# Sixteen more tokens leave the dense expert path of a mixed layer kernel: 352 columns, 160 dots, a new order of gathers

## What is computed

```python
s = jnp.einsum('thpd,hpkd->thpk', q, sub_keys)            # scores against 2 x 128 keys per head
s_top, i_top = lax.top_k(s, PEER_TOPK)                     # 16 of each half
best_s, best_pos = lax.top_k(cand_s, PEER_TOPK)            # 16 of the 256 pairs
experts = jnp.take_along_axis(cand_i, best_pos, axis=-1)
g = jax.nn.softmax(best_s, axis=-1)
act = jax.nn.gelu(jnp.einsum('thkd,td->thk', expert_u[experts], xb))
wgt = (g * act)
y = jnp.einsum('thk,thkd->td', wgt, expert_v[experts])
```

## Time and profile before

| | |
|---|---|
| median of 3 runs | 2411.23 us (2410.53 to 2413.74) |
| profiled execution, first to last instruction (the span) | 2411.4 us |
| TensorE busy | 2367.4 us (98%) |
| VectorE busy | 1567.8 us (65%) |
| GpSimd busy | 1244.2 us (52%) |
| bytes moved by DMA | 526.14 MB, mean 218 GB/s |

### The profile page before, as it was taken

The page is one execution under the profiler, slowest core; times in us unless marked ns, Lnnn a source line. Parts: engine busy times, 40 slices in busy tenths (PEclk is TensorE's granted clock), DMA queues, the critical chain, the costliest instruction groups (busy, mean ns, idle before and its releaser), DMA issues.

```text
span 2411.4 us, 35928 instructions
## 1 busy us (share of the span) xinstructions
PE 2367.4 (98%) x12892; PEld 2127.2 (88%) x12892; DVE 1567.8 (65%) x2831; ACT 945.5 (39%) x1488; POOL 1244.2 (52%) x704
## 2 busy tenths in 40 slices
PE   7999999999999999999999999999999999999998
PEld 4878887899999999999999999997777888888886
DVE  5258535689899999779999999892266225422201
ACT  4374333344455555333333333342353223332312
POOL 2305443337899999555555555444304444444443
PEclk9999999999999999999999999999999999999999
DMA  7227522327978898999999999943202222222231
GB/s 283 80 115 258 182 91 84 133 94 255 324 252 301 299 328 309 396 379 414 416 415 409 417 408 414 370 166 106 82 14 96 97 96 96 96 93 99 90 102 70
DMA packets 179613, 526.14 MB, mean 218 GB/s; under 512 B 18240, under 2 KB 70896, under 8 KB 178224
## 3 DMA queue, kind: packets, MB, share of 16 engines
q1 hardware_dynamic: 120928, 345.24, 39.7%
q0 software_dynamic: 43024, 159.14, 17.0%
q10 hardware_dynamic: 15552, 20.36, 2.4%
HBM read 474.93 MB, written 49.73 MB: 218 GB/s over the span
## 4 chain that ended last, share of the span: by engine, by line
PE 91%; DVE 3%; DMA 2%; issue 2%; POOL 1%; ACT 1%; SPq 0%; ACTq 0%; DVEq 0%; POOLq 0%
PE bank L1372 21%; PE bank L1374 21%; PE bank L1373 21%; PE pair L1373 6%; PE pair L1372 6%; PE pair L1374 6%; PE pair L1726 1%; POOL wlo L714 1%; DMA wraw<-in_w 1%; PE bank L1889 1%; PE pair L1513 1%; PE bank L1552 1%; PE bank L1539 1%; DMA act_dram<-actb 1%; PE pair L1664 1%
## 5 line engine op out<-in xcount | busy, mean ns | idle before, releaser
L714 POOL TENSOR_TENSOR wlo<-wraw,whi 128x1024 fp32r<-128x1024 f32 x303 | 740.4, 2446 | 761.1 <-ACT whi L856 760.2
L1372 PE MATMUL bank<-HH,whi 128*128 128x512 f32 (+1 forms) x2048 | 740.2, 361 | 9.5 <-DMA T<-in_keys 3.0
L1373 PE MATMUL bank<-HL,whi 128*128 128x512 f32 (+1 forms) x2048 | 735.8, 359 | 0.0
L1374 PE MATMUL bank<-HH,wlo 128*128 128x512 f32 (+1 forms) x2048 | 735.7, 359 | 0.0
L856 ACT ACTIVATE whi<-wraw 128x1024 fp32r<-128x1024 f32 x456 | 481.8, 1058 | 632.2 <-PE pair L1374 337.4
L1372 PEld LDWEIGHTS bank<-HH,whi 128*128 128x128 f32 x2048 | 385.0, 188 | 54.8 <-issue 5.7
L1374 PEld LDWEIGHTS bank<-HH,wlo 128*128 128x128 f32 x2048 | 384.5, 188 | 40.3
L1373 PEld LDWEIGHTS bank<-HL,whi 128*128 128x128 f32 x2048 | 385.0, 188 | 39.6 <-issue 0.5
L780 POOL DMA_INDIRECT VROW<-in_w,which x128 | 206.0, 1609 | 190.5 <-DVE YROW L2522 178.0
L2454 DVE TENSOR_TENSOR wlo<-wraw,whi 128x1024 fp32r<-128x1024 f32 x153 | 186.4, 1219 | 20.9 <-ACT whi L856 20.0
L773 POOL DMA_INDIRECT X<-in_u_rows,which x128 | 149.0, 1164 | 57.3 <-DVE dots L2296 32.6
(11 more groups left out here) (447 smaller groups left out, 3815.1 us busy)
## 6 DMA issues: line engine op xcount, KB each, us to landing
wraw<-in_w SPq DMA_DIRECT2D x456, 512.0 KB
gate_dram<-GS SPq DMA_DIRECT2D x24, 1024.0 KB
GJ<-gate_dram SPq DMA_DIRECT2D x32, 768.0 KB
act_dram<-actb ACTq DMA_DIRECT2D x108, 184.0 KB
AJ<-act_dram SPq DMA_DIRECT2D x108, 184.0 KB
adaw<-in_ada SPq DMA_DIRECT2D x32, 512.0 KB
ada<-in_ada SPq DMA_DIRECT2D x16, 512.0 KB, 14.2
NB<-in_nab POOLq DMA_DIRECT2D x4, 1024.0 KB
```

What stands on the lines that cost most here:

```text
L714: nc.gpsimd.tensor_tensor(wlo[:, slot, :, :].rearrange("p k c -> p (k c)"), wraw[:, slot, :, :].rearrange("p k c -> p (k c)"), whi[:, slot ...
L1372: pe.matmul(out_, ah, bh, start=first, stop=False, **kw)
L1373: pe.matmul(out_, ah, bl, start=False, stop=False, **kw)
L1374: return pe.matmul(out_, al, bh, start=False, stop=last, **kw)
```

## The change

Sixteen more tokens of the block before the last go by rows. `FT` is 32, so `SD` = 352, `STEPS` = 88, `FS` = 4 and `DOTS` = 160: a row of V for the few tokens after each third tile instead of each seventh. Of the 160 dots, 28 stay in the lead, 44 are in the gate stage (46 before), `TAIL_DOTS` = 66 in the tail (38 before) and 22 in the second stage (32 before), one in five tiles. The tail's dots are spread over the 25 tiles 103 to 127. In its first 12 tiles (103 to 114) the low halves are made by GpSimd, which puts the gathers of each tile behind them; from tile 115 on (`U_POOL`) VectorE makes them. The number of slots stays four.

```diff
-FT = 16
+FT = 32
...
-U_POOL = 4 * GATE_IT + GATE_TILES + 3
+U_TAIL = 4 * GATE_IT + GATE_TILES + 3
+U_POOL = 115
...
-GATE_DOT = 2
-PSUM_DOTS = TOP_DOTS + STEPS // GATE_DOT
-U_DOTS = 112
+GATE_DOTS = 44
+PSUM_DOTS = TOP_DOTS + GATE_DOTS
+TAIL_DOTS = 66
+U_DOTS = PSUM_DOTS + TAIL_DOTS
 DOTS = P + FT
-V_DOT_TILES = [10 * m // 3 + 1 for m in range(32)][:DOTS - U_DOTS]
+V_DOT_TILES = [5 * m + 1 for m in range(DOTS - U_DOTS)]
...
+        def gate_dots(q):
+
+            return GATE_DOTS * q // STEPS
+
...
@@ GpSimd, gate stage and tail
-                if q >= 2 * GATE_DOT and q % GATE_DOT == 0:
+                while fetched < R + TOP_DOTS + gate_dots(max(q - 2, 0)):
                     fetch_u(fetched)
                     fetched += 1
             for t in range(lows, U_POOL):
                 lo(G0["U"] + t, t % R)
-            for k in range(fetched, U_DOTS + R):
+                while fetched < R + PSUM_DOTS + (t - U_TAIL + 1) * TAIL_DOTS // (P - U_TAIL):
+                    fetch_u(fetched)
+                    fetched += 1
+            u_fetches = min(U_DOTS + R, DOTS)
+            for k in range(fetched, u_fetches):
                 fetch_u(k)
@@ VectorE, gate stage
-                if q % GATE_DOT == GATE_DOT - 1:
+                while dotted[0] < TOP_DOTS + gate_dots(q + 1):
                     dot()
@@ VectorE, tail
-            v.wait_ge(w_lo, G0["U"] + U_POOL)
-            tail_dots = U_DOTS - PSUM_DOTS
-            for t in range(U_POOL, P):
-                lo(G0["U"] + t, t % R)
-                while dotted[0] < PSUM_DOTS + (t - U_POOL + 1) * tail_dots // (P - U_POOL):
+            for t in range(U_TAIL, P):
+                if t == U_POOL:
+                    v.wait_ge(w_lo, G0["U"] + U_POOL)
+                if t >= U_POOL:
+                    lo(G0["U"] + t, t % R)
+                while dotted[0] < PSUM_DOTS + (t - U_TAIL + 1) * TAIL_DOTS // (P - U_TAIL):
                     dot()
```

More of the change, by code:

```diff
@@ L820, in _ @@
                 pool.wait_ge(g_out[b], 64 * TD)
-            fetched = U_DOTS + R
+            fetched = u_fetches
             for n, k in enumerate(V_ROWS):
```

## The result

The changed kernel takes 2462.86 us (median of 4 runs, 2460.47 to 2466.33), the kernel before 2411.28 us beside it (2410.53 to 2413.74). The ratio is 1.0212 with a 95% interval of 1.0197 to 1.0226: slower by 51.6 us, where +33.5 was forecast. Direction and range held; the likeliest value was 18 us too low.

A forecast was written before the change was run, and what follows sets the result against it. TensorE looked like the bound (98% busy), but DMA was taken to give at most 410 to 416 GB/s. From 2411.4 us, -3.5 - 8 + 41 + 4 = +33.5 gives 2445 us; range 2418 to 2480.

The forecast's parts named there:

- The lead and the gate stage: Before the tail: lead -3.5 us (bounds 0 and -6.2), gate stage -8 us (bounds -4 and -12).
- The second stage: Second expert stage: DMA at its limit, 4.09 us a tile for tiles 0 to 95, in sum +4 us.
- TensorE's pace: Rival, second stage: it keeps 3.84 us a tile, -20.5 us in place of +4, whole 2421 us; chance 0.15.
- a slot bound of 4.3 us a tile: Rival, second stage: slots of V rows bind it, +24 us, whole 2465 us; chance 0.16.
- The tail: Last VectorE gate sum to second stage: gathers wait for slots, 2.3 us a dot, 153 us, +41 us.
- the low bound: Tail: round of a less loaded DMA, 8.0 us, 2.0 a dot, 134 us, under the limit of bytes.
- the high bound: Tail: GpSimd's 12 low halves (29 us) stand between its gathers with nothing hiding them, 182 us.
- The signs: Expected: tail some 150 us, TensorE idle a third, dots 2.2 to 2.4 us apart, DMA near 400 GB/s.
- the third: Sign of being wrong: TensorE's waits in the tail bring its clock to 1.2 GHz, 7.7 us a tile, tail over 190.

The follow-up runs named there:

- ScalarE's order: Changed kernel, but ScalarE evacuates TensorE's first-stage tiles 125 to 127 before it splits the second stage's first three products: 2459.60 us.
- The square of four runs: Changed kernel 2462.86 us; with the tail's low halves all on VectorE 2446.68; with `few_x` in PSUM for dots 72 to 103 2449.43; with both 2444.22.
- the split of 38/50: Changed kernel with 38 dots in the tail, 50 in the second stage and all the tail's low halves on VectorE: 2431.16 us, ratio 1.0074.

## Why the prediction was right, and where it was too low

The direction and the path to it were right: the tail decides, by gathers that wait for slots. The size of that one term was too small.

**The lead and the gate stage**: right, -5.8 and -9.3 for -3.5 and -8. VectorE's waits for gathers in the lead fell from 7.1 us to 1.2, nearly all of what could fall, and VectorE ends the gates at 673.60, where TensorE waits for them 0.63 us. I had halved that gain.

**The second stage**: right in its limit, +0.6 for +4. Tiles 32 to 96 take (1532.4 - 1268.0) / 64 = 4.13 us where 4.09 was worked out, and 96 to 112 take 3.84, as forecast. Tiles 4 to 32 are faster, at 3.94, which the sum had at 4.09. The windows of the changed kernel above reach 414 GB/s at most. Why tiles 4 to 32 are faster stays open. Both rivals there fall: TensorE's pace, and a slot bound of 4.3 us a tile.

**The tail** is the term that was mis-sized: +67.7 for +41. The mechanism (a gather waits for the dot four before it, bytes second) was right: three slots cost 22 us, and where GpSimd makes no low halves a dot takes 2.29 us for the 2.3 worked out from the earlier trace rows. (The 0.6 us to wake GpSimd, in the low bound alone, should have been 0.36: by the same rows a gather starts 1.50 us after the start of the dot that frees its slot, and the dot is 1.14 of them.) The step that failed is the overlap on the high bound: "GpSimd's 12 low halves (29 us) stand between its gathers, and nothing hides them: 182. Most of that is hidden, since up to four gathers fly on while a low half is made." Most of it wasn't: 16.2 of the 29 us show in the whole, and the tail took 179.8. That this is so near the high bound of 182 is luck, since 4.6 us of it are ScalarE's order and 11 a collision, neither of which the bound was made of. It failed in two ways.

- The low halves cost 16.2 us. I took GpSimd's time as the price; the larger part is a price on the other engine. The earlier trace rows showed no trouble because in the gate stage the dots have one operand in PSUM. In the tail both are in SBUF, which no dot of the trace of before has beside a low half of GpSimd; but the sums at 185.78 to 263.73 have it, with up to 3.42 us in place of 1.22, and I didn't read them. The square of four runs parts this: with `few_x` in PSUM the low halves on GpSimd cost 5.2 us, without it 16.2. So some 11 of the 16 us are the collision at the operand's place (the stretched dots and the longer issues of gathers, which these runs don't part), and 5 are what is left, most likely the queue on GpSimd at the tail's start: with `few_x` in PSUM, dot 74 starts at 974.10 where a low half stands ahead of its gather and at 968.45 where none does, and dots 78 to 103 are no further apart (2.28 and 2.32).
- The ends. Of the 9.6 us at the start 6.6 are the low halves again and the rest is gather 74, which without them still takes from 960.42 to 968.36 to land, with a low half of VectorE before its dot; of the 4.8 us at the end, 4.6 are ScalarE's order. The end was read from the earlier trace rows, where TensorE still had tiles to do while VectorE finished; with TensorE run dry, the same order is exposed.

Without the low halves on GpSimd the kernel was measured at 2446.68, against 2445 forecast. That it comes so near is partly luck: its tail takes 162.4 us where the sum had 153, and the lead (-6.3), the gate stage and the second stage (-2.4 for +4) make up for it.

**The signs** that I gave: TensorE idle for 29% of the tail (a third, said), dots 2.29 and 2.79 us apart (2.2 to 2.4), 333 GB/s (near 400; 389 with the low halves on VectorE in its first 92 us), matmuls of 352 columns from 675.83 to 677.60 in 11 steps of 0.161 us (0.160). Of the signs of being wrong, no window shows over 425 GB/s and no stretch of dots comes at under 1.8 us, but the third came in part: TensorE's granted clock did fall to the level of 1.2 GHz around waits in the tail (0.88 in the mean), and the tail stayed under 190. A tile at that level takes 24 x 0.293 = 7.0 us, not the 7.7 of the forecast, which had doubled the 0.160.

No version here beats the kernel before. The 16 tokens save TensorE 41 us of work at most, and 32 more gathers of 0.52 MB cost 40 us at 415 GB/s in stages where the DMA is at 391 to 413 already. Only the lead and the gate stage gain, 15 us, and in the gate stage, at 300 GB/s, VectorE and GpSimd are full.

## What to carry to other kernels

Before a cost is taken from one stage, look for the same pair of operations elsewhere in the trace: an operation whose mean is far above its shortest (here 2.15 us for 1.21) is where such a price shows. When work is moved to GpSimd, don't price it by GpSimd's idle time alone: look whether VectorE's instructions beside it have both inputs in SBUF, and if so, count each overlap as a stall of one of the two, or put one operand in PSUM. When an engine-bound stage becomes bound by another, read every in-order wait at its two ends again: what stood behind TensorE's tiles for free now stands on the path. And a stage at the transfers' limit pays the full bytes of all that is moved to it, whoever does the work.

## What the runs showed of the hardware

A dot of VectorE with two SBUF operands took up to 4.04 us beside a low half of GpSimd, which takes 2.4, and 1.22 with one of the operands in PSUM beside the same low halves. GpSimd's issue of an indirect gather took 1.51 us in the mean among the first kind of dot and 0.94 among the second, with the same bytes. The tail of the run with `few_x` in PSUM has both kinds: 34 issues that overlap a VectorE instruction with both inputs in SBUF take 0.94 to 1.98 us, 1.44 in the mean, and the 38 others 0.93 to 0.96. In the kernel before it is so too: 1.88 and 1.68 us in the tail, beside dots and low halves with both inputs in SBUF, and 0.95 in the lead.

TensorE's granted clock fell again and again in the tail, to 0.50 in some windows, during or after waits for low halves:

```profile
999.44 0.66 PE L1382 MATMUL bank<-HH,whi 128*128 128x352 f32 x1 [3.70 <-POOL wlo L720]
999.89 0.49 PE L1383 MATMUL bank<-HL,whi 128*128 128x352 f32 x1
1000.19 0.49 PE L1384 MATMUL bank<-HH,wlo 128*128 128x352 f32 x1
1000.48 0.49 PE L1382 MATMUL bank<-HH,whi 128*128 128x352 f32 x1
```

```profile
1000.00:1004.00 4.00, 4.00 (x15) 4.00 (x14) 2.46 (x4) 0.00 (x0) 1.43 (x2) 0.50 1.04 419
```

The matmuls stand 0.29 us apart and not 0.161: the level of 1.2 GHz, after an idle time of 3.70 us. From 1004.84 on they are back at 0.16. In the split of 38/50, whose tail has no such waits, the clock is 1.00 throughout. TensorE had been waiting for low halves before these slow tiles, so I don't count them as the bound, but a tile at that level takes 7.0 us and the tail gives each 7.2. No run here sets the clock apart from the waits; what it adds stays open.
